# HGRN state keys: decay scans and block transposes on VectorE and a turn through DRAM, in place of TensorE transposes

## What is computed

```python
    decay = jnp.exp(jnp.where(causal[:, :, None], rel, -jnp.inf))
    scores = jnp.einsum('bhtk,bhsk,bhtsk->bhts', q, k, decay)
    o = scores @ v + einsum(q * exp(bcum), S)
    S_new = exp(b_end)[..., None] * S + einsum('bhsk,bhsv->bhkv', k * exp(b_end[:, :, None, :] - bcum), v)
```

## Time and profile before

| | before |
|---|---|
| median of 3 runs | 1538.14 us (1537.91 to 1538.66) |
| profiled execution, its own time | 1538.48 us |
| its span in the trace | 1536.7 us |
| granted TensorE clock over the span | 0.999 |

### The profile page before, as it was taken

One profiled execution on the slowest core, in us unless ns is written; L12 is line 12 of the kernel. 1 busy time (PEld: TensorE's weight loads), 2 busy tenths in 40 slices (PEclk: granted clock), 3 DMA queues, 4 the chain that ended last, 5 costly groups with the idle time before them and its releaser, 6 DMA issues.

```text
span 1536.7 us, 29779 instructions
## 1 busy us (share of the span) xinstructions
PE 1524.7 (99%) x12343; PEld 1366.3 (89%) x12343; DVE 1050.5 (68%) x1750; ACT 577.3 (38%) x1038; POOL 362.4 (24%) x333
## 2 busy tenths in 40 slices
PE   9999999999999999999999999999999999999998
PEld 9999999999998899889998898888888988888887
DVE  6656565775767678676887678779615787787246
ACT  5323222353344244434444445472112246541121
POOL 0000000030422124032332224434430044343510
PEclk9999999999999999999999999999999999999999
DMA  5322322323333334323334233554324334452331
GB/s 172 111 83 86 104 86 83 111 83 103 99 110 88 110 96 128 111 84 97 99 112 139 70 121 108 155 164 138 102 90 138 110 103 151 148 168 83 125 122 55
DMA packets 151859, 170.75 MB, mean 111 GB/s; under 512 B 6348, under 2 KB 122480, under 8 KB 151728
## 3 DMA queue, kind: packets, MB, share of 16 engines
q1 hardware_dynamic: 119728, 138.71, 28.8%
q10 hardware_dynamic: 31920, 29.97, 6.6%
q0 software_dynamic: 80, 0.20, 0.0%
HBM read 151.82 MB, written 17.04 MB: 110 GB/s over the span
## 4 chain that ended last, share of the span: by engine, by line
PE 57%; DVE 3%; issue 0%; ACT 0%
PE acc L416 16%; PE acc L417 16%; PE acc L418 16%; PE aux L418 1%; PE aux L417 1%; PE aux L416 1%; PE aux L1421 1%; DVE xns L2568 1%; PE aux L577 1%; PE aux L644 1%; PE aux L646 1%; PE aux L1439 1%; PE aux L1440 0%; PE aux L1387 0%; DVE yal L2558 0%
## 5 line engine op out<-in xcount | busy, mean ns | idle before, releaser
L416 PE MATMUL acc<-xhis,whi 128*128 128x264 f32 (+2 forms) x1848 | 608.8, 329 | 0.0
L417 PE MATMUL acc<-xlos,whi 128*128 128x264 f32 (+2 forms) x1848 | 602.0, 326 | 0.0
L418 PE MATMUL acc<-xhis,wlo 128*128 128x264 f32 (+2 forms) x1848 | 601.9, 326 | 0.0
L416 PEld LDWEIGHTS acc<-xhis,whi 128*128 128x128 f32 x1848 | 348.0, 188 | 29.3 <-issue 0.3
L418 PEld LDWEIGHTS acc<-xhis,wlo 128*128 128x128 f32 x1848 | 347.9, 188 | 29.3
L417 PEld LDWEIGHTS acc<-xlos,whi 128*128 128x128 f32 x1848 | 348.2, 188 | 27.0
L411 POOL TENSOR_TENSOR wlo<-raw,whi 128x1024 fp32r<-128x1024 f32 x84 | 208.4, 2483 | 366.0 <-DVE whi L2613 366.0
L407 ACT ACTIVATE whi<-raw 128x1024 fp32r<-128x1024 f32 x158 | 164.0, 1048 | 131.5 <-PE acc L418 119.3
L411 DVE TENSOR_TENSOR wlo<-raw,whi 128x1024 fp32r<-128x1024 f32 x81 | 99.8, 1235 | 36.9 <-ACT whi L407 36.7
L2291 DVE TENSOR_TENSOR wlo<-raw,whi 128x1024 fp32r<-128x1024 f32 x77 | 95.0, 1235 | 27.3 <-ACT whi L407 27.1
L2613 DVE CAST whi<-raw 128x1024 fp32r<-128x1024 f32 x84 | 61.2, 733 | 54.0 <-PE acc L418 53.8
(11 more groups left out here) (394 smaller groups left out, 2782.9 us busy)
## 6 DMA issues: line engine op xcount, KB each, us to landing
raw<-in_w_in SPq DMA_DIRECT2D x38, 1024.0 KB, 5.3
raw<-in_hgrn_w_in SPq DMA_DIRECT2D x32, 1024.0 KB, 5.8
raw<-in_pool_w_in SPq DMA_DIRECT2D x15, 1024.0 KB, 5.6
raw<-in_pool_w_out SPq DMA_DIRECT2D x8, 1024.0 KB, 4.9
raw<-in_hgrn_w_out SPq DMA_DIRECT2D x8, 1024.0 KB, 4.9
raw<-in_w_out SPq DMA_DIRECT2D x8, 1024.0 KB, 4.9
v_turn<-vb ACTq DMA_DIRECT2D x8, 544.0 KB, 2.7
raw<-in_pool_w_grp SPq DMA_DIRECT2D x4, 1024.0 KB, 5.1
```

The source lines that it names most:

```text
L416: pe.matmul(dst, stat[0], mov[0], start=first, stop=False)
L417: pe.matmul(dst, stat[0], mov[1], start=False, stop=False)
L418: return pe.matmul(dst, stat[1], mov[0], start=False, stop=last)
```

## The change

The state keys no longer come out of the chain of levels. DVE makes the decays with four backward scans for each head while the pair is projected (`decays`, behind units 2 and 3), POOL multiplies the keys by them once, DVE turns 32x32 blocks (`keys_blocks`, behind units 6 and 7), ACT sends them to DRAM in unit 1 of the next phase (`keys_out`), SP fetches them (`keys_in`), and ACT puts them in the order that S_KV wants at the start of unit 4 (`keys_placed`). S_KT is gone from PE and ACT, and level 7 of `k_times` from POOL. The eviction of i0 on DVE now waits for `kt_ready`, because the keys travel through the buffer of the i units.

```diff
+                        ibs = sb("ibs", [P, 2, T], where=in_b)
+                        ib = [ibs[:, x, :] for x in range(2)]
...
+            def kd_of(pair):
+                return fbs[0] if pair == 2 * NG - 1 else ibs
...
-            for x in range(2):
+            for x in range(2 if s > S_KT else 0):
                 big, small = aux2[:, x, :], aux[:, x, :]
-                if s == S_KT:
-
-                    pe.wait_ge(k_step, k_after(pair, LEVELS, x))
-                    pe.wait_ge(sc_done, read(pair, GROUPS - 1, x) - 2)
-                    for c in range(CH - 1):
-                        pe.transpose(small[:, P * c:P * c + P],
-                                     k1[x][:, META + P * c:META + P * c + P], ident[:, :])
-                    pe.transpose(small[0:META, 3 * P:4 * P], kb[par][x][:, 0:META], ident[:, :])\
-                      .then_inc(kt_full, 1)
-                elif s == S_KV:
-
-                    pe.wait_ge(kt_ready, 4 * pair + 2 * x + 2)
+                if s == S_KV:
+
+                    pe.wait_ge(kt_ready, 2 * pair + x + 1)
+                    pe.wait_ge(kt_landed, 80 * pair + 80)
...
-            elif s == S_KT:
-                for x in range(2):
-                    act.wait_ge(kt_full, 2 * pair + x + 1)
-                    act.activation(kt[x][:, :, :], aux[:, x, 0:3 * P].rearrange("p (c d) -> p c d", c=3),
-                                   ACT.Copy).then_inc(kt_ready, 1)
-                    act.activation(ktm[x][0:META, :], aux[0:META, x, 3 * P:4 * P], ACT.Copy).then_inc(kt_ready, 1)
...
+            def keys_in(pair):
+                sp.wait_ge(kd_sent, 16 * pair + 16)
+                if pair == 0:
+                    sp.wait_ge(m_zero, 4)
+                else:
+                    sp.wait_ge(kv_full, 2 * pair)
+                cols = k_turn.rearrange("(a p) x t -> p x a t", a=4)
+                w = 32 * (CH - 1)
+                for b in range(4):
+                    sp.dma_start(kts_of(pair)[32 * b:32 * b + 32, :, :, :], cols[:, :, :, w * b:w * b + w])\
+                      .then_inc(kt_landed, 16)
+                sp.dma_start(ktms[0:META, :, :].rearrange("p x (a j) -> p x a j", a=4), cols[0:META, :, :, 4 * w:4 * w + 32])\
+                  .then_inc(kt_landed, 16)
...
-                    turn_at[count + (2 if part == "last" else 4)] = (values_in, n_pair)
+                    turn_at.setdefault(count + (2 if part == "last" else 4), []).append((values_in, n_pair))
+                    turn_at.setdefault(count + 4, []).append((keys_in, n_pair))
...
-                        for x in range(2):
+                        for x in range(2 if g == 0 else 0):
+                            pool.wait_ge(decay_ready, 2 * pair + x + 1)
+                            pool.tensor_tensor(snb[x][:, 0:KEYS], kb[par][x][:, 0:KEYS], snb[x][:, 0:KEYS], ALU.mult)\
+                                .then_inc(kd_ready, 1)
+                        for x in range(2 if g < GROUPS - 1 else 0):
                             pool.wait_ge(sc_full, scored(pair, g, x))
                             k_times(2 * g + 1, x)
...
+                    if process is not None and j == 4:
+                        keys_placed(process[0])
                     side()
                     side()
...
+                    if process is not None and j == 1:
+                        keys_out(process[0])
...
+            def keys_out(pair):
+                act.wait_ge(kd_blocks, 2 * pair + 2)
+                if pair:
+                    act.wait_ge(kt_landed, 80 * pair)
+                act.dma_start(k_turn[:, :, :], kd_of(pair)[:, :, 0:SEQ - P + 32]).then_inc(kd_sent, 16)
+
+            def keys_placed(pair):
+                act.wait_ge(kt_landed, 80 * pair + 80)
+                if pair:
+                    act.wait_ge(zblo_ready, 2 * pair)
+                else:
+                    act.wait_ge(sq_summed, KT - 1)
+                for x in range(2):
+                    act.activation(kt[x].rearrange("p c (a j) -> p c a j", a=4),
+                                   kts_of(pair)[:, x, :, :].rearrange("p a (c j) -> p c a j", c=CH - 1), ACT.Copy)                       .then_inc(kt_ready, 1)
...
                 if s == 0:
                     outputs_in(2 * NG - 2)
+                    keys_out(2 * NG - 1)
+                if s == S_KT:
+                    keys_placed(2 * NG - 1)
...
+                def decays(x):
+                    dve.wait_ge(f_ready, 2 * pair + x + 1)
+                    dve.wait_ge(k_ready, 1 + 2 * pair + x + 1)
+                    if part == "first" and x == 0:
+                        dve.wait_ge(none_ready, 1)
+                    dve.memset(snb[x][:, META - 1:KEYS:P], 1.0)
+                    for c in range(CH):
+                        lo, hi = (META + P * (c - 1), META + P * c) if c else (0, META)
+                        done = dve.tensor_tensor_scan(snb[x][:, lo:hi - 1][:, ::-1], fb[par][x][:, lo + 1:hi][:, ::-1],
+                                                      spare[:, 2:3].to_broadcast([P, hi - lo - 1]), 1.0,
+                                                      ALU.mult, ALU.max)
+                    done.then_inc(decay_ready, 1)
+
+                def keys_blocks(x):
+                    dve.wait_ge(kd_ready, 2 * pair + x + 1)
+                    dve.wait_ge(vb_ready, 4 * pair + 2 * x + 2)
+                    dve.transpose(kd_of(pair)[:, x, 0:SEQ - P].rearrange("p (b c j) -> p c b j", b=4, c=CH - 1),
+                                  snb[x][:, META:KEYS].rearrange("p (c b j) -> p c b j", c=CH - 1, b=4))
+                    dve.transpose(kd_of(pair)[:, x, SEQ - P:SEQ - P + 32], snb[x][:, 0:32]).then_inc(kd_blocks, 1)
...
                             if x == 0:
                                 if part != "first":
                                     dve.wait_ge(vb_sent, 16 * pair)
+                                    dve.wait_ge(kt_ready, 2 * pair)
...
                     if j:
                         finish(j - 1)
+                    if j in (2, 3):
+                        decays(j - 2)
+                    if j in (6, 7):
+                        keys_blocks(j - 6)
```

More of the change, by code:

```diff
@@ L208, in program @@
         with ExitStack() as in_b:
-            fb, kb, gb = [], [], []
+            fbs, fb, kb, gb = [], [], [], []
             q_second = sb("q_second", [P, 3, SEQ], where=in_b)
@@ L215, in program @@
                     if name == "gb" and p == 0:
-                        ib = [sb(f"ib{x}", [P, T], where=in_b) for x in range(2)]
+                        ibs = sb("ibs", [P, 2, T], where=in_b)
+                        ib = [ibs[:, x, :] for x in range(2)]
                     if name == "gb" and p == 1:
@@ L219, in program @@
                         sb("vts_room", [P, 2 * META], where=in_b)
-                    bufs.append([sb(f"{name}{p}{x}", [P, w], where=in_b) for x in range(2)])
+                    if name == "fb":
+                        fbs.append(sb(f"fbs{p}", [P, 2, T], where=in_b))
+                        bufs.append([fbs[p][:, x, :] for x in range(2)])
+                    else:
+                        bufs.append([sb(f"{name}{p}{x}", [P, w], where=in_b) for x in range(2)])
             qall = [q_first, q_second]
@@ L236, in program, with kts_of @@
             vtm = [vtms[:, x, :] for x in range(2)]
+            def kd_of(pair):
+                return fbs[0] if pair == 2 * NG - 1 else ibs
+            def kts_of(pair):
+                rows = kd_of(pair)[:, :, :].rearrange("p x t -> p (x t)")
+                return rows[:, 0:2 * (SEQ - P)].rearrange("p (x a n) -> p x a n", x=2, a=4)
             kt = [sq[x][:, 0:SEQ - P].rearrange("p (c d) -> p c d", c=CH - 1) for x in range(2)]
-            ktm = [sb(f"ktm{x}", [P, P], where=in_b) for x in range(2)]
+            ktms = sb("ktms", [P, 2, P], where=in_b)
+            ktm = [ktms[:, x, :] for x in range(2)]
             st = [sb(f"st{x}", [P, CH, P], where=in_b) for x in range(2)]
@@ L345, in program @@
         tb_step, q_copied, k_copied = sem("tb_step"), sem("q_copied"), sem("k_copied")
-        kt_full, kt_ready = sem("kt_full"), sem("kt_ready")
+        none_ready, decay_ready, kd_ready = sem("none_ready"), sem("decay_ready"), sem("kd_ready")
+        kd_blocks, kd_sent, kt_landed = sem("kd_blocks"), sem("kd_sent"), sem("kt_landed")
+        kt_ready = sem("kt_ready")
         kv_full, st_ready = sem("kv_full"), sem("st_ready")
@@ L483, in k_after, with k_made @@
             return 2 * LEVELS * pair + 2 * (level - 1) + x + 1
+        def k_made(pair, level, x):
+            return 2 * (LEVELS - 1) * pair + 2 * (level - 1) + x + 1
         def copied(pair, g, x):
@@ L539, in program @@
         v_turn = nc.dram_tensor("v_turn", (P, 2, SEQ + 32), F32).ap()
+        k_turn = nc.dram_tensor("k_turn", (P, 2, SEQ - P + 32), F32).ap()
+        KEYS = META + SEQ - P
         S_VT, S_KT, S_KV, S_O, S_ON = 0, 1 + GROUPS, 2 + GROUPS, 3 + GROUPS, 4 + GROUPS
@@ L598, in group_wait @@
```

(10 more changed lines are left out.)

## The result

The changed kernel takes **1547.57 us** (median of 6 runs, 1547.31 to 1549.48) against 1538.23 for the kernel before (6 runs, 1537.91 to 1538.66). The ratio is 1.0064, 95% interval 1.0054 to 1.0074: slower by 9.3 us. The changed kernel's profiled execution took 1549.48 us, 1.9 above the median, with a span of 1547.7. The prediction was 1540.0 with a range to 1546.5 and "no change" as the likeliest; it was wrong.

The account below looks back on a forecast made before the run. PE, busy 99%, was taken as the bound, with DVE's serial chain to S4 in even phases. Even phases +4.8, odd and last phases -3.5, tail +0.6 gave +1.9 on 1538.14: 1540.0 us, range 1536.5 to 1546.5.

Parts of the forecast that it names:

- "no change": Outcome within 0.2% (3.1 us) of the kernel before, given chance 0.52.
- "The rest": ACT, SP and POOL side work, transfer and clock: SP's wait for the sending and the keys' landing have slack; cost nothing.
- "The transfer is late": Rival, slower: i0's eviction and S_KV wait for the keys, 7 us per further microsecond, 1547 at one; chance 0.04.
- S_KT, 0.88 us a pair: On PE, dropping S_KT's transposes saves 0.88 us a pair, at most 7.0 us over seven phases and the tail.
- The scans, d = 1.3 us a head: On DVE, between S1 and S_KV: a head's memset and four scans cost 1.3 us, between 0.8 and 1.8.
- Even phases, +1.6 each: DVE's scans delay S4 and its copies, so S_KV starts at 484.3, not 482.71: +1.6 us, three times, +4.8.
- "a head dearer than 1.43 us breaks it": Odd and last phases: S_KV holds with 0.25 us to spare, winning 0.88 each (-3.5), unless a head exceeds 1.43 us.
- Tail: PE already waits for DVE's states before S_O: S_KT's gain 0, `keys_blocks` adds 0.6, L644's wait grows to about 1.4.
- The hidden rival: Rival, faster: DVE's decays are hidden and PE keeps all 7.0 us it saves, 1531 us; chance 0.08.

Follow-up runs that it names:

- e1: Changed kernel with SP's `keys_in` two weight loads later in the odd phases behind an output projection: 1539.06 us, ratio 1.0003 to the kernel before.
- e4: Kernel before the change, with every S_KT transpose on PE made twice: 1544.64 us, ratio 1.0038.
- e3: Changed kernel with `keys_in` two loads later behind an output projection and both heads' scans behind unit 5: 1534.33 us, ratio 0.9971.
- e6: Changed kernel with scans behind unit 5 and, for pairs behind an output projection, ACT's key sending moved into that projection: 1534.21 us, ratio 0.9974.
- e9: e7 with 64 already fulfilled waits in front of PE's program: 1537.39 us, ratio 0.9995.
- e7: e6 with SP's fetch of the values one load earlier in even phases behind an odd one: 1534.11 us, ratio 0.9974.
- e2: Changed kernel with both heads' scans moved on DVE from behind units 2 and 3 to behind unit 5: 1539.83 us, ratio 1.0013.

## Why the prediction was wrong

**The step that failed** is in "The rest": "the sending goes out in unit 1 and at 2.7 us, like `v_turn`, is over before SP's turn". That was read from one odd phase, the first, where SP's turn comes behind unit 1. `turn_at` counts weight loads, and `count` grows by two more for an output projection, whose loads come first; so in odd phases 2 and 3 the fourth load behind the pair is only the second of the phase, and SP is there at 512.4, 24.4 us ahead of the fetch. The prediction had asked the right question (what is queued behind the wait: the next weight load) and answered it from the one kind of phase in which it is harmless. Of its rivals, "The transfer is late" is the nearest, but it named the eviction of i0 and S_KV, which were not late; the weights were. It had 0.04.

Put against the sum, in us of the two profiled executions:

| term | forecast | measured |
|---|---|---|
| odd phase 1 | -0.88 | -0.89 |
| odd phases 2 and 3 | -1.76 | +8.65 |
| three even phases | +4.8 | +3.10 |
| last phase and tail | -0.88 + 0.6 | -0.34 + 0.13 |
| ahead of the first S1 | 0 | +0.35 |
| sum | +1.9 | +11.0 |

So one term is off by 10.4 us. With e1, which repairs it alone, the kernel is 0.4 us above the kernel before where +1.9 was forecast; the even phases, dearer by 3.4 us in all and not by 4.8, make up the difference. Some of the 8.65 may be of this execution only: it is 1.9 us above the median, and the stretch at half the clock costs up to 1.4 (odd phase 2 against odd phase 3, whose stands are 0.2 shorter in all). Whether other executions have that stretch is not shown; their mean granted clock is 0.996 to 0.998, this one's 0.998.

**S_KT, 0.88 us a pair**: right, by odd phase 1 and by e4.

**The scans, d = 1.3 us a head**: the size was wrong, too high for the head whose scans run alone and too low for the one beside POOL. The scans of odd phase 1, head 0 and head 1 on DVE, and POOL at the same time:

```profile
409.63 0.17 DVE L2310 TENSOR_TENSOR_SCAN snb<-fbs,spare 128x15 f32<-128x15 f32 x1
...
409.73 1.02 DVE L2310 TENSOR_TENSOR_SCAN snb<-fbs,spare 128x127 f32<-128x127 f32 x3
...
417.22 0.38 DVE L2310 TENSOR_TENSOR_SCAN snb<-fbs,spare 128x15 f32<-128x15 f32 x1
...
417.52 2.00 DVE L2310 TENSOR_TENSOR_SCAN snb<-fbs,spare 128x127 f32<-128x127 f32 x3
```

```profile
416.70 1.42 POOL L1122 TENSOR_TENSOR tb<-tb 128x132 f32<-128x132 f32 x2
418.08 1.16 POOL L1142 TENSOR_TENSOR snb<-kb,snb 128x400 f32<-128x400 f32 x1
```

Head 0, beside an idle POOL, takes 1.04 us (409.63 to the next pass at 410.67), 0.34 for 127 elements, inside the 0.30 to 0.40 named. Head 1 runs beside POOL's products and takes 2.2 us (417.22 to 419.45), with 2.00 for the three long scans; above 0.5 us a scan is a sign of being wrong that the prediction had named. The pair's 3.2 us stand against 2.6. Which head is slow changes with the phase: in odd phases 2 and 3, where DVE is late, it is head 0 (2.3 us) and not head 1 (1.1), and in even phases it is head 1 (2.0), by its short scan alone. The half throughput of the Trainium skill ("DVE: opcode table, instruction layouts, handler registers and perf-mode slots", section 6) agrees with head 0: the estimate from it had (1.2 - 0.2) / 3 = 0.33 us for a scan of 127 elements, and 0.34 was measured. The Trainium skill's rule on shared SBUF interfaces ("GPSIMD Engine Reference", table of the engine), which the prediction had weighed for L700, agrees with head 1: the scan has two SBUF inputs, and beside POOL it takes about twice as long.

**Even phases, +1.6 each**: +1.04, +0.97, +1.09. The mechanism is the one forecast: PE waits at S4 in two of the three (1.5 us each; in even phase 2 the stand without releaser comes first) and at S_KV for DVE's copies of S4. Even phase 1, PE:

```profile
475.59 0.30 PE L589 MATMUL aux<-q_first,kb 128*32 128x32 f32 x13 [1.46 <-DVE ab L700]
...
483.17 0.46 PE L646 MATMUL aux<-vtms,ktms 128*128 128x128 f32 x2 [0.65 <-DVE ab L696]
```

and DVE:

```profile
474.94 0.43 DVE L700 COPY_PREDICATED ab<-masks,aux 128x256 f32<-128x256 int32 x1
...
482.43 1.21 DVE L696 COPY ab<-aux 64x128 f32<-64x128 f32 x4
```

S4 starts 25.20 us behind S1 (475.59 - 450.39), before 24.13, so 1.07 later where 1.3 was said. The rest of the error is one reading: the prediction let S_KV wait until DVE had copied S4 of both heads. The code waits for one head at a time (`read(pair, GROUPS - 1, x)`), and S_KV starts at 483.17, ahead of the end of the four copies at 483.64. Half of 1.21 is 0.6 us, which is forecast minus measured. The same misreading made "a head dearer than 1.43 us breaks it" wrong: in odd phase 1 the four copies end at 423.86 + 1.21 = 425.07, later than said, and S_KV still starts when it is due, at 425.30 (DVE, then PE):

```profile
423.86 1.21 DVE L696 COPY ab<-aux 64x128 f32<-64x128 f32 x4
```

```profile
425.30 0.38 PE L646 MATMUL aux<-vtms,ktms 128*128 128x128 f32 x2
```

**Tail**: L656 waits 0.9 us, not 1.4, and the transposes behind unit 7 cost the 0.6 forecast, nearly: DVE needs 0.59 us for them (840.85 to 841.44), and the last phase loses 0.54 of its 0.88.

**The hidden rival** (1531 us, 0.08) needed a chain in which S3 is not late. The changed kernel does not have it; e3 builds it, by moving the scans past S4, and is 4.4 us below the kernel before (1534.33 against 1538.69 in the runs beside it). Of what is missing to 7.0, the stands of 1.03 and 1.54 us are the greater part: in the traces the span is 3.9 us shorter, and would be 6.5 shorter without them. The rest lies in the last phase and the tail, which win about 0.4 each and not 0.88.

## What to carry to other kernels

When a wait is put on a queue that also issues other transfers, find where the wait falls in every kind of phase, not in one: here the same line is harmless in one odd phase and holds a weight load back in the two others (24 us of waiting, the load 21 us later), because its place is counted in loads and an output projection has loads of its own. Move the producer of what is waited for ahead (e6) or the wait behind the urgent loads (e1). And put new work of an engine that is not the bottleneck where that engine's own idle time is: the same scans cost 4.7 us more in front of S4 than behind it (e1 against e3).

## What was not expected of the hardware

A scan on DVE slows beside POOL's products. In odd phase 1 head 0's 15 elements take 0.17 us alone. In even phase 1 head 1's 15 take 1.02 us while POOL multiplies, and the three scans of 127 behind them, with POOL done at 477.09, take no more than head 0's:

```profile
476.12 1.02 DVE L2310 TENSOR_TENSOR_SCAN snb<-fbs,spare 128x15 f32<-128x15 f32 x1
...
477.06 1.02 DVE L2310 TENSOR_TENSOR_SCAN snb<-fbs,spare 128x127 f32<-128x127 f32 x3
```

```profile
475.60 1.49 POOL L1142 TENSOR_TENSOR snb<-kb,snb 128x400 f32<-128x400 f32 x1
```

PE can stand with no semaphore to explain it: 0.58 to 1.61 us, 14 times in the phases of the nine traces with the change in them (waits under 0.35 us not counted), at places that move when PE's program is shifted (e9). All 14 have two things in common. Count PE's instructions in the trace (matmuls, weight loads, semaphore instructions): at each stand 193 or 194 more than a multiple of 256 have started. And PE goes on 1.25 to 1.58 us after a packet of 16 KB of the queue `q8 instruction` has come in (start and duration of the packet in the trace; in e7 it comes in at 592.53 and PE goes on at 594.04). An execution has 98 such packets, and e7's trace has 25122 PE instructions, 256 for each. So PE stands where the next packet of its own program begins. What makes that packet late is not shown. Around the stand of e7 the DMA engines are busy for 0.78 to 0.98 of the time, but at e9's second, whose packet comes in from 470.37 to 471.43, the DMA share is 0.03, behind 0.92 from 460 to 465 us; and most of the 98 places are passed without a stand, in the kernel before all of those in its phases.

The granted clock of PE fell to 0.50 in the changed kernel's trace behind stands of 1.67 and 2.28 us with 7 us of full work between them. Stands of 1.79, 0.58 and 1.38 us in odd phase 3 of the same trace, and of 1.88 us in e2's, left it at 1.00. In e6 and e7 it is at 0.50 once more from 1528 to 1530 us, where PE has no matmul.
